# A two-block layer on one core: a new opening, w_ada dealt evenly, attention maps copied by one engine, and three products that end half by half

## The reference

```python
# block 1
mod = silu(c) @ w_ada + b_ada                 # 2048 -> 6 x 2048: shift_a, scale_a, gate_a, shift_f, scale_f, gate_f
h = rms_norm(x, g_attn_pre) * (1 + scale_a) + shift_a
proj = h @ w_in                               # 5456 columns: q, k, v of two attentions and an indexer
mixed = concat(differential_attention, indexed_sparse_attention) @ w_o
x = x + gate_a * rms_norm(mixed, g_attn_post)
h = rms_norm(x, g_ffn_pre) * (1 + scale_f) + shift_f
x = x + gate_f * rms_norm((silu(h @ w_gate) * (h @ w_up)) @ w_down, g_ffn_post)
# block 2
h = rms_norm(x, pre_norm_g_2)
proj = h @ w_in_2                             # low-rank q and kv, gates, convolution inputs
y_mla = (causal attention, 16 heads, times silu(z)) @ w_o_mla_2
y_conv = (b_gate * conv3(c_gate * c_in) * silu(z_conv)) @ w_o_conv_2
out = (sigmoid(g_mla) * y_mla + sigmoid(g_conv) * y_conv) @ w_out_2
x = x + rms_norm(out, post_norm_g_2)
```

## Time and profile before

| | us |
|---|---|
| runs shown | 2403.37, 2403.71, 2404.49 |
| median | 2403.71 |
| the profiled execution, its own time | 2403.83 |
| its span, first to last instruction | 2402.5 |
| TensorE busy | 2288.5 |
| VectorE busy | 1400.4 |
| ScalarE busy | 1065.3 |

### The profile page before, as it was taken

The page is one execution under the profiler, slowest core; times in us unless marked ns, Lnnn a source line. Parts: engine busy times, 40 slices in busy tenths (PEclk is TensorE's granted clock), DMA queues, the critical chain, the costliest instruction groups (busy, mean ns, idle before and its releaser), DMA issues.

```text
span 2402.5 us, 26312 instructions
## 1 busy us (share of the span) xinstructions
PE 2288.5 (95%) x10768; PEld 1858.3 (77%) x10768; DVE 1400.4 (58%) x1903; ACT 1065.3 (44%) x1471; POOL 0.7 (0%) x5
## 2 busy tenths in 40 slices
PE   4899989889999999999998999999999999999998
PEld 2676767777888888888887878888888888888886
DVE  1459999795775464554456554545544554554554
ACT  2333544444444444434444555555444444444443
POOL 0000000000000000000000000000000000000000
PEclk7999999998999999999999999999999999999999
DMA  7888678593786675556553744444565555555553
GB/s 295 332 321 297 228 263 305 196 357 123 272 281 219 202 253 190 180 194 195 187 193 118 237 149 154 149 154 153 193 193 193 186 184 193 191 191 195 180 188 140
DMA packets 255455, 505.69 MB, mean 210 GB/s; under 512 B 9077, under 2 KB 19662, under 8 KB 254182
## 3 DMA queue, kind: packets, MB, share of 16 engines
q1 hardware_dynamic: 255334, 504.00, 62.2%
HBM read 499.77 MB, written 4.19 MB: 210 GB/s over the span
## 4 chain that ended last, share of the span: by engine, by line
PE 86%; DVE 7%; ACT 3%; DMA 2%; issue 1%; SPq 0%; DVEq 0%; ACTq 0%
PE bank L595 27%; PE bank L597 26%; PE bank L596 26%; DVE wlo L1674 2%; PE bank L611 2%; DMA raw<-in_w_in_dram 2%; DVE acc L1655 1%; PE bank L679 1%; ACT whi L1062 1%; DMA raw<-in_w_ada_dram 1%; PE bank L549 1%; PE bank L619 1%; DVE x L1726 0%; PE bank L702 0%; PE bank L531 0%
## 5 line engine op out<-in xcount | busy, mean ns | idle before, releaser
L1674 DVE TENSOR_TENSOR wlo<-raw,whi 128x1024 fp32r<-128x1024 f32 (+2 forms) x760 | 912.8, 1205 | 871.9 <-ACT whi L1062 870.2
L1062 ACT ACTIVATE whi<-raw 128x1024 fp32r<-128x1024 f32 (+2 forms) x760 | 789.9, 1044 | 1037.9 <-PE bank L597 917.5
L595 PE MATMUL bank<-whi,Ahi 128*128 128x512 f32 (+2 forms) x2304 | 910.8, 395 | 33.6 <-DVE wlo L1674 22.2
L596 PE MATMUL bank<-wlo,Ahi 128*128 128x512 f32 (+2 forms) x2304 | 896.6, 389 | 0.0
L597 PE MATMUL bank<-whi,Alo 128*128 128x512 f32 (+2 forms) x2304 | 896.4, 389 | 0.0
L595 PEld LDWEIGHTS bank<-whi,Ahi 128*128 128x128 f32 x2304 | 437.3, 190 | 132.9 <-DVE wlo L1674 31.9
L597 PEld LDWEIGHTS bank<-whi,Alo 128*128 128x128 f32 x2304 | 437.2, 190 | 90.2
L596 PEld LDWEIGHTS bank<-wlo,Ahi 128*128 128x128 f32 x2304 | 437.9, 190 | 83.4
L1655 DVE SCALAR_TENSOR_TENSOR acc<-raw,cs,acc 128x512 f32<-128x512 f32 x224 | 157.2, 745 | 0.1
L595 PE MATMUL bank<-whi,Fhi 128*128 128x512 f32 x352 | 137.6, 391 | 0.0
L597 PE MATMUL bank<-whi,Flo 128*128 128x512 f32 x352 | 137.1, 389 | 0.0
(11 more groups left out here) (291 smaller groups left out, 1344.3 us busy)
## 6 DMA issues: line engine op xcount, KB each, us to landing
raw<-in_w_in_dram SPq DMA_DIRECT2D x156, 1024.0 KB, 5.0
raw<-in_w_ada_dram SPq DMA_DIRECT2D x96, 1024.0 KB, 6.8
raw<-in_w_gate_dram SPq DMA_DIRECT2D x44, 1024.0 KB, 5.1
raw<-in_w_up_dram SPq DMA_DIRECT2D x44, 1024.0 KB, 5.1
raw<-in_w_down_dram SPq DMA_DIRECT2D x44, 1024.0 KB, 5.0
raw<-in_w_o_dram SPq DMA_DIRECT2D x16, 1024.0 KB, 6.7
raw<-in_w_o_mla_dram SPq DMA_DIRECT2D x16, 1024.0 KB, 4.9
raw<-in_w_o_conv_dram SPq DMA_DIRECT2D x16, 1024.0 KB, 4.9
```

The lines of the kernel that those rows point to most:

```text
L595: pe.matmul(o, a_hi, w_hi, start=beg, stop=False)
L596: pe.matmul(o, a_hi, w_lo, start=False, stop=False)
L1062: act.activation(m.whi[:, i % NHL, :, 0:n], m.raw[:, c % NRAW, 2 * h:2 * h + 2, 0:n], ACT.Copy).then_inc(m.s_hi, 1)
L1674: dve.tensor_tensor(m.wlo[:, i % NHL, :, 0:n], m.raw[:, c % NRAW, 2 * h:2 * h + 2, 0:n], m.whi[:, i % NHL, :, 0:n].bitcast(F32), ALU.subtr ...
```

## The change

- Host side: small inputs are laid out as columns before the launch, and x is also given turned (`x_turned`). Two turns by TensorE go, eleven small loads become a few.
- Opening: loads are issued as columns, first w_ada chunk, constants, second w_ada chunk, turned x in two, and so on. Turned x is squared by ScalarE in two pieces, summed over its blocks by VectorE, over partitions by TensorE with ones. Scale is applied ahead of shift; ScalarE writes `Ahi` with the shift as bias, VectorE `Alo` with the shift added. No turn of x by TensorE in the four quarters. x itself is loaded later, in four pieces, behind w_in's chunks.
- w_ada's chunks are dealt as `DEAL_PE` and `DEAL_VECTOR` say, and those on TensorE are put half behind the first unit of a chunk and half behind the second.
- ScalarE copies both maps.
- In the last column group of w_o, w_down and w_out_2 (`skew`), the last three units' products for the second token half are held back until the first half is complete, which `s_half` signals. `last_pass` keeps splits of the next matrix behind the norm, and `resume` lets them go. Norms, additions and the final stores go by token half.

```diff
-BETWEEN, BETWEEN_LAST = (3, 3, 2, 0, 0), (1, 1, 1, 1, 2)
-W_IN_SHARE = 26
+DEAL_PE = ((3, 3, 2, 2, 1), (2, 2, 1, 1, 1), (2, 2, 2, 0, 0), (0, 0, 0, 0, 0))
+DEAL_VECTOR = ((0, 0, 0, 0, 0), (0, 0, 0, 1, 1), (0, 0, 0, 1, 1), (1, 1, 1, 1, 2))
+W_IN_SHARE = 24
...
+    def last_pass(self, n):
+        self.hold = self.unit + n - 1
+    def resume(self):
+        self.hold = len(LIN) - 1
+        self.split_to(UNIT_AT[LIN[self.unit]])
...
+                ins = products(i, ka0, 0, beg, fin)
+                if skew and 2 * (len(ks) - 1 - j) + 1 - h < 3:
+                    held.append((i, ka0))
+                    if fin:
+                        ins.then_inc(m.s_half, 1)
+                        for unit, at in held:
+                            products(unit, at, 1, False, unit == i).then_inc(m.s_mm, 1)
+                    return
+                ins = products(i, ka0, 1, beg, fin)
                 ins.then_inc(m.s_mm, 1)
+                c = LIN[i][0]
+                some = ada_beside(c) // 2
+                if h == 0:
+                    ada_products(c + 1, some)
+                else:
+                    ada_products(c + 1 + some, ada_beside(c) - some)
...
# ScalarE, opening
+    for h, o in enumerate((m.sq[:, :, :], m.tmpA[:, :, :, :].rearrange("p a k t -> p (a k) t"))):
+        need.wait_ge(m.s_xT[h], 16)
+        act.activation(o, m.xT[:, 8 * h:8 * h + 8, :], ACT.Square).then_inc(m.s_sq, 1)
...
+                ins = act.activation(m.Ahi[:, kb, :], m.tmpA[:, q % 2, kk, :], ACT.Identity, bias=m.modT[:, kb:kb + 1])
...
-            copy_out(ln.ET[:, 0:384], b0, ex[0], m.bank[b0][:, 0:384])
+            for mm, b in enumerate(ln.bank[0:nm]):
+                copy_out(ln.ET[:, 384 * mm:384 * mm + 384], b, ex[mm], m.bank[b][:, 0:384])
...
# ScalarE, after w_o
-    root(m.ssq[:, :, 0], m.rstd[:, :], D)
-    for tb in range(2):
-        for q in range(4):
-            ins = square_part(m.x, m.xn2, tb, q, 4 * tb + q + 1)
...
+    need.wait_ge(m.s_half, 1)
+    post_squares(m.y1, 3, s, 0)
+    half_root(0)
+    for q in range(4):
+        ins = square_part(m.x, m.xn2, 0, q, q + 1)
...
+        if q == 1:
+            need.wait_ge(m.s_mm, end_o)
+            post_squares(m.y1, 3, s, 1)
+        if q == 2:
+            half_root(1)
...
# VectorE, opening
+        dve.tensor_reduce(m.red[:, h, :], i.rearrange("p k t -> p t k"), AX_X, ALU.add).then_inc(m.s_red, 1)
...
+            ins = dve.scalar_tensor_tensor(out=m.tmpA[:, q % 2, kk, :], in0=m.xT[:, kb, :], scalar=m.gs[:, kb:kb + 1],
+                                           in1=m.rstdT[:, :], op0=ALU.mult, op1=ALU.mult)
...
# VectorE, after w_o
+    post_half(m.y1, s, 0)
+    for q in range(4):
+        post_part(m.y1, 0, q)
+    post_half(m.y1, s, 1)
+    post_part(m.y1, 1, 0)
     need.wait_ge(m.s_sq, k.up(m.s_sq))
+    half_sum(0)
+    post_part(m.y1, 1, 1)
+    half_inverse(0)
+    diagonal(0)
+    for q in (2, 3):
+        post_part(m.y1, 1, q)
+    need.wait_ge(m.s_sq, k.up(m.s_sq))
+    half_sum(1)
+    half_inverse(1)
+    diagonal(1)
+    k.resume()
...
# VectorE, after w_down
+            need.wait_ge(m.s_half, 2)
+            add(0)
+            need.wait_ge(m.s_y2sq, 7)
+            half_sum(0)
+            gain(0)
+            half_inverse(0)
+            for q in range(3):
+                post_part(m.y2, 0, q)
+            need.wait_ge(m.s_mm, k.unit)
+            add(1)
+            post_part(m.y2, 0, 3)
...
     def block2_operand(q):
-        for tb in range(2):
-            post_part(m.y2, tb, q)
+        post_part(m.y2, 1, q)
+        if q == 0:
+            k.resume()
...
# SyncE
+        if c in at_x:
+            tb, h = divmod(at_x.index(c), 2)
+            need.wait_ge(m.s_shlo, 8)
+            cols = slice(1024 * h, 1024 * h + 1024)
+            sp.dma_start(x[:, tb, cols], A["x"][0, tb * P:tb * P + P, cols]).then_inc(m.s_x, 16)
...
+    pieces = ((0, 0, 2048, 4), (1, 0, 1024, 6), (1, 1024, 1536, 7), (1, 1536, 2048, 8))
+    for i, (tb, c0, c1, parts) in enumerate(pieces):
+        need.wait_ge(m.s_xp, 16 + parts)
+        sp.dma_start(m.out[0, tb * P:tb * P + P, c0:c1], x[:, tb, c0:c1]).then_inc(m.s_end[i], 16)
```

More of the change, by code:

```diff
@@ L59, in lin @@
         plan.append(("lin", w, k0, c0, n))
[L61 to L64, removed]
+    first = [("ada", g, j) for g in ADA_ON_PE for j in range(4)]
+    rest = [("ada", g, j) for g in range(8, 20) for j in range(4)]
+    plan += first[:8]
+    del first[:8]
     for q in range(4):
@@ L67, in chunk_plan @@
             lin("w_in", 4 * q, *win_cols(cg))
-            n = (BETWEEN if q < 3 else BETWEEN_LAST)[i]
-            plan += rest[:n]
-            del rest[:n]
+            for some, n in ((first, DEAL_PE[q][i]), (rest, DEAL_VECTOR[q][i])):
+                plan += some[:n]
+                del some[:n]
+    assert not first
     late = len(rest)
@@ L162, with ada_beside @@
 UNIT_AT = {u: i for i, u in enumerate(UNITS)}
+def ada_beside(c):
+    n = 0
+    while c + n + 1 < len(PLAN) and PLAN[c + n + 1][0] == "ada" and c + n + 1 not in ADA_NO:
+        n += 1
+    return n
 def unit_after(w, k0, c0):
@@ L536, in ada_take, with ada_products @@
             ins.then_inc(m.filled[b], 1)
-    def ada_products(c):
-        while c < len(PLAN) and PLAN[c][0] == "ada" and c not in ADA_NO:
+    def ada_products(c, n, beside=None):
+        for c in range(c, c + n):
             _, g, j = PLAN[c]
@@ L557, in ada_columns @@
         need.wait_ge(m.freed[b], k.use(b) - 1)
[L558 removed]
+        acc = m.sums[:, idx % 2, :]
         for fb in range(4):
@@ L574, in linear, with products @@
         hi_a, lo_a = operand
+        held = []
+        def products(i, ka0, tb, beg, fin):
+            for kk in range(2):
+                o = m.out_bank(s, tb, n)
+                xs = slice(tb * P, tb * P + P)
+                a_hi, a_lo = hi_a[:, ka0 + kk, xs], lo_a[:, ka0 + kk, xs]
+                w_hi, w_lo = m.whi[:, i % NHL, kk, 0:n], m.wlo[:, i % NHL, kk, 0:n]
+                pe.matmul(o, a_hi, w_hi, start=beg and kk == 0, stop=False)
+                pe.matmul(o, a_hi, w_lo, start=False, stop=False)
+                ins = pe.matmul(o, a_lo, w_hi, start=False, stop=fin and kk == 1)
+            return ins
         for j, k0 in enumerate(ks):
@@ L633, in turn_quarter, with beside @@
         turn_block(5, x_block, k0 + 2, True)
[L637 to L643, removed]
-    k.split_to(UNIT_AT[LIN[1]])
[L647 to L651, removed]
+    k.split_to(UNIT_AT[LIN[1]])
+    def beside(idx, j):
+        if (idx, j) == (1, 0):
+            need.wait_ge(m.s_const, 16)
+            k.use(4)
+            for h in range(2):
+                need.wait_ge(m.s_red, h + 1)
+                ins = pe.matmul(m.bank[4][:, 0:S], m.ones, m.red[:, h, :], start=(h == 0), stop=(h == 1))
+            ins.then_inc(m.filled[4], 1)
+        if (idx, j) == (1, 2):
+            ada_columns(0)
     def shifted(base):
@@ L892, in tensor_program @@
         for g in range(4):
+            last = third is THIRDS[2] and g == 3
+            if last:
+                k.last_pass(6)
             linear("w_down", 512 * g, 512, m.F_op, lambda q, h: freed(F_at[q][h]), ks=ks, kbase=ks[0],
-                   before=lambda j: k.finish_side() if j == len(ks) - 1 else None)
+                   before=lambda j: k.finish_side() if j == len(ks) - 1 else None, skew=last)
+    k.resume()
     A_at = {}
@@ L1045, in tensor_program @@
         linear("w_out_2", 512 * g, 512, m.A_op, operand_at(M_at),
-               before=lambda j: k.finish_side() if g == 0 and j == 3 else None)
+               before=lambda j: k.finish_side() if g == 0 and j == 3 else None, skew=(g == 3))
     assert k.unit == len(LIN)
```

417 lines of the change are left out of this document (236 added, 181 removed).

## The result

The changed kernel takes 2367.86 us (median of 4 runs, 2366.87 to 2368.85) where the kernel before took 2403.72: ratio 0.985, interval 0.9833 to 0.9867. The forecast was 2368.8, range 2358 to 2382. The profiled execution is the fastest of the four: its span is 2365.6 us, where before had 2402.5, so the profiles are 36.9 us apart and the medians 35.9.

A forecast was written before the change was run, and what follows sets the result against it. TensorE, busy 95% of the span, was taken as the bound, with about 114 us idle to win from. Terms 12.2 + 2.5 + 4 + 7.1 + 2.9 + 2.2 + 4.1 = 35.0 off 2403.83 gave 2368.8 us, range 2358 to 2382.

The forecast's parts named there:

- Opening: Start to first w_in product: earlier first load and less work behind the eighth chunk bring it to 36.5, gain 12.2 us.
- Rival (e): Opening: strided reductions of turned x are slow; from 24.8 us each the whole gain is gone, 27 gives 2408.1; chance 0.02.
- Quarters: First three quarters of w_in: x turns off PE, four VectorE w_ada chunks added to the loads; gain 2.5 us.
- The queue is not full here: First three quarters of w_in: load queue share 0.84, 20 us free, so 10.3 us of added loads largely fit.
- Rival (c): First three quarters of w_in: PE pays for the extra loads, -4.3 us instead of +2.5, total 2375.6; chance 0.16.
- Rest of w_in and w_o: 179 to 534 us: VectorE is the bound at first and four w_ada chunks leave the stretch; gain 4 us.
- Maps: Block 2's attention pairs: ScalarE copying the second map saves 1.0 us in each of seven waits, gain 7.1 us.
- Seam after w_o: Norm by halves and skewed end let PE restart at T + 7.4 instead of T + 10.3; gain 2.9 us.
- After w_down: Seam after w_down: 0.8 us at the seam and 0.7 off each of two later stalls; together 2.2 us.
- Tail: After w_out: norms by half and earlier, smaller stores end at T + 7.4 instead of T + 11.5; gain 4.1 us.
- rival (d): Seams and tail: the halves don't come early and these give nothing, total 2378.0; chance 0.07.
- rival (b): DVE-bound stretch gives back 12 us instead of 4, and PE's clock in the first quarters 5; total 2355.8; chance 0.14.

The follow-up runs named there:

- Run 4: Changed kernel with positions and lambdas loaded in six small loads ahead of the sixth w_ada chunk, as before the change: first w_in product +5.2 us, end +5.1 us.
- run 3: Changed kernel with positions and lambdas loaded ahead of the sixth w_ada chunk, still in two merged loads: 2366.18 us in one run; first w_in product +2.3.
- run 7: Changed kernel with the w_ada chunks for TensorE loaded only in half from the ninth on, part of the sums left out: end -9.4 us.
- run 5: Changed kernel with the old w_ada deal, no VectorE chunk in the first three quarters and 26 among w_in's other columns: span +4.65 us.
- run 1: Changed kernel with VectorE copying the second map again, in both blocks: span 2378.1 us, +12.5.
- run 2: Changed kernel with no products of the last three units held back; norms, additions and stores still by half: span 2371.9 us, +6.3.
- run 6: Changed kernel with VectorE's w_ada sums in w_in over 256 of 512 columns, the other half left out: end -10.9 us.
- runs 10 and 11: Changed kernel with VectorE's 24 w_ada chunks among w_in's other columns dealt unevenly, doubles behind chunks 14, 18, 21 (10; median 2368.64 us) or 14, 15 (11; end +2.8).
- runs 1, 7 and 8: The third of these, 8: changed kernel with all w_ada products behind a chunk's second w_in unit instead of half between the two: span +3.6 us.

## Why the prediction came out right, point by point

**Opening: 12.2 forecast, 12.3 measured, by the steps named.** The first load lands at 7.4, not 6.4, the eighth chunk is multiplied at 30.90 (30.3), and what follows takes 5.5 (6.2). Run 4 shows the share of the positions' and lambdas' loads, 5.2 (2.9 by merging and 2.3 by their later place, run 3); the earlier first issue (4.84 to 1.17) is 3.7 and what is gone behind the last chunk 3.3, both from timelines only. The cover for the squares was much thinner than said: a reduction takes 3.68 (at most 3.3 forecast), the product by ones waits its turn behind a w_ada product and takes 2.08, the reciprocal 1.75, and the end comes 2.0 us before it is wanted, not over 8. Rival (e) was refuted by R = 3.68, but its threshold of 24.8 was reckoned without that turn.

**Quarters: 2.5 forecast, 3.6 measured, for a wrong reason.** "The queue is not full here" is the step that failed: with the four added chunks it is full (0.97), and run 7 shows that loads bound the quarters. Rival (c) was argued away by free queue time that was not there afterwards. It came out cheap all the same, since the even deal uses the queue better (run 5: equal arrival with 4 MB less). The 3.6 are then not the deal's; the turns that are gone are the likely source, but no run puts them back. The Trainium skill's figure weighed at the opening ("DMA: Bandwidth & Descriptors", Where 436 GB/s comes from), about 358 GB/s, doesn't hold here: 368 GB/s over 126.6 us of the quarters. By it the total was to be 2372.2, and the four runs lie below that.

**Rest of w_in and w_o: 4 forecast, 3.75 measured, made of other parts.** The forecast wanted the low-split waits between 245 and 325 shorter. They aren't: 5.7 us before, 5.6 in the answering 82 us after. The 3.1 us lost in the first four units are PE's group sum that the deal moves there (run 5). From then on VectorE sets the pace as before, and the gain stays at 12.8 to 12.9 for 28 units. Then PE gains 6.8 up to T of w_o. Run 5 assigns the parts: its T of w_o is 4.5 later, so the deal gives 4.5 of this stretch. Run 5 against the kernel before is all else of the change, 15.9 ahead at the fourth quarter and 15.2 at T of w_o (534.48 against 519.31): the reload of x, ScalarE's copies in block 1 and the rest together cost 0.8. The 4.15 that undoing block 1's copies costs in run 1 can't be added to this, since before the change PE did not wait there. How the 0.8 splits stays open; no run takes the reload of x out.

**Maps: 7.1 forecast, 6.8 measured**, with one wait of 1.7 and six near 0.39, as written. Mis-placed was the other half of it: the copies of block 1 were put into the 4 us above without a price of their own, and undoing them costs 4.15 in the changed kernel.

**Seam after w_o: 2.9 forecast, 3.1 measured.** PE's idle time is 6.79 where 7.4 was forecast, and the feared late low split didn't come. The holding back itself gives 2.4 (run 2); the rest is put down to the norms by half, which no run undoes. **After w_down: 2.2 and 2.9**; idle 3.44 (4.1), stalls of 0.34, 0.98 and 0.95 (0.9). **Tail: 4.1 and 4.4**, end at T + 7.1 (T + 7.4). Holding back gives 2.6 of it; the rest is put down to smaller stores and norms, which no run undoes. The section of the Trainium skill that the forecast drew on ("DMA: Bandwidth & Descriptors", Anatomy of one DMA) is on DMAs that GpSimd issues. The last two stores of 256 KB here, which SyncE issues, landed 2.65 and 2.56 us after their issue, so its 2.6 fits. That the halves would not come early, rival (d), is refuted by the timelines; rival (b)'s 12 us behind 179 are refuted too, but run 6 shows that there were at least 10 to have.

The terms' errors are +0.1, +1.1, -0.25, -0.3, +0.2, +0.7 and +0.35: small, but partly luck, as two of the mechanisms were wrong: the free queue in the quarters, and the shorter low-split waits behind them.

## What to carry to other kernels

Free time of a queue or an engine in the profile of before is free only until the change fills it: where a change adds loads to a stretch at 0.84, ask what the share will be afterwards, and test the bound by taking work away. Where two stretches with different bounds follow each other, price an edit at the end of the second: run 5 and the changed kernel begin it at the same moment and leave it 4.5 us apart, while the 9 us that run 7 gains in the first are all but kept. Work dealt about within a full engine's stretch gained nothing (runs 10 and 11). Merge tiny loads first: six of them cost 5 us here, and none of it was made up later.

## What the runs showed of the hardware that was not expected

- A reduction of 2048 elements to 256 in each of 128 rows, eight at a time with a step of 1 KB, takes 3.68 us, near the price by neighbouring elements (8 x 0.418 = 3.3); a reciprocal of 128x256 takes 1.75 us, where adds of 512 elements take 0.7.
- Identical code behind the same seam ran at a granted clock of 0.76 or 1.00 over two units, 2.1 us apart, when its start was shifted by some us; the same happened in runs 1, 7 and 8 (7.4 us each). Seam savings of 2 us can be hidden or feigned by that.
- All but identical plans differ by up to 3.3 us at the fourth quarter (162.5 to 165.8); in the latest of them the granted clock of the third is 0.91, in the others 0.96. Behind 163 the difference stays, and the median of the changed kernel is 1.0 above its profiled run.
